# Five held weight slots, earlier turns, and low halves on ACT and GpSimd between the stages of a hybrid block

## The reference

```python
def first_block(...):
    ...
    h_res = h_res + rms_norm(m @ w_o[i], post_norm_g[i])      # 272 rows, 16 of them dropped at the end

def second_block(x, ...):
    for i in range(2):                                        # i = 0: GLA mixer, i = 1: MoBA mixer
        ...
        x = layer_norm_2(DEEPNORM_ALPHA * x + y, ln_g[i, 0], ln_b[i, 0])
        x = layer_norm_2(DEEPNORM_ALPHA * x + swiglu_ffn(x, ffn_w_gu[i], ffn_w_down[i]), ln_g[i, 1], ln_b[i, 1])
    return x

def swiglu_ffn(x, w_gu, w_down):
    gate, up = jnp.split(x @ w_gu, 2, axis=-1)
    return (jax.nn.silu(gate) * up) @ w_down
```

## Time and profile before

| | us |
|---|---|
| median of 3 launches | 913.05 |
| lowest and highest | 911.45, 913.55 |
| the profiled launch: its own time | 914.35 |
| the profiled launch: span from first to last instruction | 912.6 |
| PE busy in that span | 887.5 (97%) |
| DVE, ACT, POOL busy | 598.0, 422.0, 120.3 |
| mean granted clock of PE | 0.993 of full speed |

### The profile page before, as it was taken

How to read it: one execution, slowest core, us unless ns; L and a number is a source line. 1 busy time by engine, 2 the same in 40 slices (tenths; PEclk the granted TensorE clock), 3 DMA queues, 4 the chain that set the end, 5 groups by cost and what they waited for, 6 DMA issues and landing times.

```text
span 912.6 us, 14066 instructions
## 1 busy us (share of the span) xinstructions
PE 887.5 (97%) x5927; PEld 805.7 (88%) x5927; DVE 598.0 (66%) x845; ACT 422.0 (46%) x600; POOL 120.3 (13%) x106
## 2 busy tenths in 40 slices
PE   9999998999999999999999999989999999999995
PEld 7997998998887988879999988879977799999884
DVE  5997995687485684777555554576876765555436
ACT  5645453456652774526444443335553454444320
POOL 0343430122000311002000000015420200000000
PEclk9999998999999999999999999999999999999998
DMA  9753664563354752447665555466543656555631
GB/s 300 239 169 99 192 188 124 177 185 116 93 173 121 240 182 93 139 138 231 185 185 184 186 185 187 137 206 200 170 140 117 203 188 186 185 185 185 190 110 46
DMA packets 116009, 154.18 MB, mean 169 GB/s; under 512 B 5392, under 2 KB 91819, under 8 KB 115915
## 3 DMA queue, kind: packets, MB, share of 16 engines
q1 hardware_dynamic: 114218, 148.31, 51.9%
q0 software_dynamic: 1728, 4.98, 2.0%
HBM read 151.44 MB, written 1.05 MB: 167 GB/s over the span
## 4 chain that ended last, share of the span: by engine, by line
PE 87%; DVE 9%; ACT 1%; issue 1%; DMA 1%; DVEq 0%; SPq 0%
PE acc L572 25%; PE acc L573 24%; PE acc L574 24%; DVE w_lo L1548 2%; DVE conv L1693 2%; PE acc L637 2%; PE acc L638 1%; PE acc L640 1%; PE misc L708 1%; DVE y L1979 1%; PE misc L770 1%; ACT x_hi L1335 1%; PE acc L610 1%; DVE sc_acc L1713 1%; DMA x<-in_x 1%
## 5 line engine op out<-in xcount | busy, mean ns | idle before, releaser
L1548 DVE TENSOR_TENSOR w_lo<-staged,w_hi 128x1024 fp32r<-128x1024 f32 (+1 forms) x274 | 334.2, 1244 | 148.7 <-ACT w_hi L1140 147.8
L572 PE MATMUL acc<-x_hi,w_hi 128*128 128x256 f32 (+1 forms) x1288 | 367.5, 285 | 3.0 <-DVE m L1772 3.0
L573 PE MATMUL acc<-x_lo,w_hi 128*128 128x256 f32 (+1 forms) x1288 | 365.1, 283 | 0.0
L574 PE MATMUL acc<-x_hi,w_lo 128*128 128x256 f32 (+1 forms) x1288 | 362.6, 281 | 0.0
L1140 ACT CAST w_hi<-staged 128x1024 fp32r<-128x1024 f32 (+1 forms) x274 | 277.5, 1044 | 81.7 <-DMA staged<-in_ffn_w_down 46.8
L572 PEld LDWEIGHTS acc<-x_hi,w_hi 128*128 128x128 f32 x1288 | 243.0, 189 | 5.7 <-DVE m L1772 3.2
L574 PEld LDWEIGHTS acc<-x_hi,w_lo 128*128 128x128 f32 x1288 | 245.0, 190 | 0.0
L573 PEld LDWEIGHTS acc<-x_lo,w_hi 128*128 128x128 f32 x1288 | 243.6, 189 | 0.7 <-issue 0.2
L574 PE MATMUL acc<-w_hi,h_lo 128*128 128x512 f32 x176 | 69.6, 396 | 0.0
L572 PE MATMUL acc<-w_hi,h_hi 128*128 128x512 f32 x176 | 69.6, 395 | 0.0
L573 PE MATMUL acc<-w_lo,h_hi 128*128 128x512 f32 x176 | 69.6, 395 | 0.0
(11 more groups left out here) (371 smaller groups left out, 1197.8 us busy)
## 6 DMA issues: line engine op xcount, KB each, us to landing
staged<-in_ffn_w_gu SPq DMA_DIRECT2D x88, 512.0 KB, 3.6
staged<-in_w_in SPq DMA_DIRECT2D x58, 512.0 KB, 3.6
staged<-in_ffn_w_down SPq DMA_DIRECT2D x44, 512.0 KB, 4.1
staged<-in_gla_w_in SPq DMA_DIRECT2D x24, 512.0 KB, 3.7
staged<-in_moba_w_in SPq DMA_DIRECT2D x24, 512.0 KB, 3.9
staged<-in_w_o SPq DMA_DIRECT2D x8, 512.0 KB, 3.8
staged<-in_gla_w_out SPq DMA_DIRECT2D x8, 512.0 KB, 3.6
staged<-in_moba_w_out SPq DMA_DIRECT2D x8, 512.0 KB, 3.6
```

Of the source, the lines that this page charges most:

```text
L572: pe.matmul(dst, st_hi, mv_hi, start=start, stop=False)
L573: pe.matmul(dst, st_hi, mv_lo, start=False, stop=False)
L574: return pe.matmul(dst, st_lo, mv_hi, start=False, stop=stop)
L1548: nc.vector.tensor_tensor(lo, raw, hi, ALU.subtract).then_inc(split, 1)
```

## The change

1. `TAIL` becomes 5. In `n_product` the fourth slot of column half 0 is held too: after three slots for both tiles come slot 3 for tile 0, slots 4 to 7 for tile 0, and then slots 3 to 7 for tile 1. One semaphore, `tail_part`, counts the finished accumulators.
2. Turn 0 is issued inside the old stage, ahead of the last held slot of tile 1 (in `down0`: ahead of the last two slots of tile 1's half 1). Turn 1 opens `n_first`. Turn 2 stands between the two groups of low-half matmuls of tile 0, and turn 3 behind them. Within a tile all sixteen matmuls with `x_hi` now come ahead of the eight with `x_lo`.
3. The filler matmuls ahead of turns 0 and 2 are gone.
4. The low halves of tile 0 leave DVE: ACT copies the turned bank to `y` right behind the rounding, and POOL subtracts `x_hi` from it into `x_lo`.
5. The inverse root has one second-order step and one third-order step: five small instructions behind the seed in place of six, with other constants in the gain. In `w_o` two further small instructions become one.
6. DVE no longer takes column half 0 of both tiles in the middle of its weight splits, nor tile 1's half 0 inside tile 0's norm: `tail_norms` first norms tile 0 whole, and then takes tile 1. In `w_o` ACT's squares move in the same way.

```diff
@@ n_first
+                turn_rows(tag, 1)
                 open_out(name)
                 done = 4 * (int(tag[1]) - 1)
                 for t in range(TILES):
                     rows = slice(t * P, t * P + P)
-                    turn_rows(tag, 2 * t, 2)
-                    for j in range(2):
-                        pe.wait_ge(s["x_rounded"], done + 2 * t + j + 1)
-                        for part in range(2):
-                            if part == 1:
-                                if j == 0:
-                                    turn_rows(tag, 2 * t + 1, 0)
-                                await_read(pe, "%s_%d" % (tag, 2 * t + j))
+                    for part in range(2):
+                        for j in range(2):
+                            if part == 0:
+                                pe.wait_ge(s["x_rounded"], done + 2 * t + j + 1)
+                            elif t == 0:
+                                if j == 1:
+                                    turn_rows(tag, 2)
+                                pe.wait_ge(s["x_rest"], done // 2 + j + 1)
+                            else:
+                                await_read(pe, "%s_%d" % (tag, 2 + j))
...
+                    if t == 0:
+                        turn_rows(tag, 3)
@@ n_product
+                for q in range(3):
                     chunks_ready(q)
                     n_slots(stage, names, st_hi, st_lo, q, q + 1)
+                chunks_ready(3)
+                quarter(3, 0)
                 open_out(names[1])
...
+                for i in range(4, 8):
+                    quarter(i, 0)
+                for i in range(3, 8):
+                    if i == 7:
+                        turn_rows(tag, 0)
+                    quarter(i, 1)
@@ swiglu, PE
                             if t == 0 and hf == 0:
                                 down_ready(k)
+                            if layer == 0 and t == 1 and hf == 1 and k == FCH - 2:
+                                turn_rows("x3", 0)
                             mm = down_half(k, t, hf)
@@ ACT
+            for hf in range(2):
+                act.wait_ge(s["tail_part"], PARTS["w_o"] + hf + 1)
+                act.wait_ge(s["m_split"], 4)
+                squares(0, hf).then_inc(s["wo_ssq"], 1)
+            slot_done(act, "w_o", 3)
+            squares(1, 0).then_inc(s["wo_ssq"], 1)
...
+                if t == 0:
+
+                    nc.scalar.copy(y[:, 0, j * 512:j * 512 + 512], bank(name)).then_inc(read_sem(name), 1)
 
             def after_tail(stage, tag):
 
                 last = FIRST[stage] + COUNT[stage] - 1
+                round_rows(tag, 0)
+                if stage == "w_o":
+                    slot_done(act, "w_o", 7)
+                    squares(1, 1).then_inc(s["wo_ssq"], 1)
+                round_rows(tag, 1)
                 lead(Slot(last - 1, 0))
-                round_rows(tag, 0)
-                round_rows(tag, 1)
+                round_rows(tag, 2)
                 lead(Slot(last, 0))
-                round_rows(tag, 2)
                 round_rows(tag, 3)
@@ DVE
+                n = count(nc.vector.tensor_scalar(r.bitcast(I32), v.bitcast(I32), -0.5, ROOT_SEED, ALU.mult, ALU.add))
+                beside(0)
                 dve.wait_ge(dve_chain, n)
...
+                n = count(nc.vector.scalar_tensor_tensor(t, r, v, r, ALU.mult, ALU.mult))
+                beside(1)
+                dve.wait_ge(dve_chain, n)
+                link(nc.vector.scalar_tensor_tensor(r, t, -ROOT_A, r, ALU.add, ALU.mult))
+                link(nc.vector.scalar_tensor_tensor(t, r, v, r, ALU.mult, ALU.mult))
+                link(nc.vector.scalar_tensor_tensor(t, t, -ROOT_B, t, ALU.add, ALU.mult))
+                link(nc.vector.scalar_tensor_tensor(r, t, ROOT_C, r, ALU.add, ALU.mult))
...
+            def tail_norms(k, stage, first_half_done):
+
+                names = TAIL_OUTS[stage]
+                for hf in range(2):
+                    dve.wait_ge(s["tail_part"], PARTS[stage] + hf + 1)
+                    residual_moments(0, names[hf], hf)
+                norm_tile(k, 0)
+                first_half_done()
+                residual_moments(1, names[0], 0)
+                slot_done(dve, stage, COUNT[stage] - 1)
+                residual_moments(1, names[1], 1)
+                norm_tile(k, 1)
@@ POOL
+            def rest_tile0(tag):
+
+                for j in range(2):
+                    await_read(pool, "%s_%d" % (tag, j))
+                    nc.gpsimd.tensor_tensor(x_lo[:, 4 * j:4 * j + 4, 0:P], y[:, 0, j * 512:j * 512 + 512]
+                                            .rearrange("p (c r) -> p c r", c=4), x_hi[:, 4 * j:4 * j + 4, 0:P].bitcast(F32),
+                                            ALU.subtract).then_inc(s["x_rest"], 1)
```

163 lines of the change are left out of this document (56 added, 107 removed).

## The result

| | before | changed |
|---|---|---|
| median, us | 913.16 (4 launches) | 902.81 (4 launches, 900.99 to 904.25) |
| ratio, 95% interval | | 0.9889 [0.9867, 0.9911] |
| profiled launch: own time, span | 914.35, 912.6 | 904.15, 902.4 |
| granted clock of PE, share of full speed | 0.993 | 0.992 |

The change makes the kernel 10.4 us faster. The prediction was 895.3 with a range up to 900.5: some 7.5 us of the forecast gain are missing.

The account below looks back on a forecast made before the run. PE, busy 887.5 of 912.6 us, was taken as the bound. Four places save 17.8, less 2.55 of waits at turn 2, plus 2.45 at the end: 17.7 us, giving 895.3 us against the median of 913.05; range 892.3 to 900.5.

Parts of the forecast that it names:

- PE as the bound: Whole kernel: PE works 887.5 of 912.6 us, so only its idle time and unused work can shorten it much.
- the stretches at the four places: Behind w_o, gla_out, down0 and moba_out: 69.47 us falls to 4 x 12.9 = 51.6 with turns unwaited, saving 17.8.
- the wait at turn 2: PE waits 0.85 us for tile 1's x behind gla_out, down0 and moba_out, 2.55 in all; none counted in w_o.
- no wait of PE for weights: Inside the stages: PE never waits for splits or loads; the rival that weights are the limit, near 913, has chance 0.02.
- the end: Program's end: the last x starts 4.43 to 4.5 us behind PE's end in place of 6.94, gaining 2.45.
- "Just in time" for turn 0: Behind the old stage's held matmuls: x due at T + 5.24, or 5.6 behind gla_out and moba_out; turn at T + 5.6.
- the first rival (turn 0 late): Late x stops the six held matmuls too: about 2.1 us each behind gla_out and moba_out, 899.5 us; chance 0.10.
- the clock rival: Without fillers and with waits at turn 2, PE's clock falls once or twice: 898.4 to 901.5 us; chance 0.12.
- The 0.7 for POOL beside DVE: In tile 1's norm: POOL's subtraction slows DVE's two centrings to 0.57 of their pace, losing 0.7 us a place.
- Weight loads: The extra held slot frees 5.6 us later; load, rounding and split take 6.0, hidden with some ten us of cover.

Follow-up runs that it names:

- e2: The changed kernel with ACT's first copy of q for MoBA moved ahead of the weight cast queued there; 902.92 us, ratio 0.9880.
- e6: The changed kernel with four slots in place of five kept for tile 1 in down0 and down1; 905.66 us, ratio 0.9926.
- e13: e11 plus POOL's second subtraction of tile 0 waiting for tile 1's second centring, behind gla_out, down0 and moba_out; 897.72 us, ratio 0.9830.
- e1: The changed kernel with tile 1's low-half matmuls in n_first in pairs again, ahead of the next high-half ones; 896.49 us, ratio 0.9832.
- e4: The changed kernel with POOL issuing the swap of k ahead of its rotation of q, for all pairs of heads; 898.93 us, ratio 0.9838.
- e11: The changed kernel with the swap of k issued ahead of POOL's rotation of q for the first two MoBA heads alone; 897.63 us, ratio 0.9831.
- e12: The changed kernel with both e1's pairs and e11's early swap of k for the first two heads; 896.91 us, ratio 0.9821.
- e14: The kernel before with ACT copying MoBA's first two heads of q five times in place of once; 920.12 us, ratio 1.0064.
- e15: The changed kernel with SP holding the twelfth MoBA q and k weight load until the first swap of q has landed; 903.55 us, ratio 0.9890.
- e3: The changed kernel with the third load of gain and shift moved behind the MoBA swaps; 901.36 us, ratio 0.9857.

## Why the prediction was wrong

**Right, by its steps.** PE as the bound; the stretches at the four places (12.90, 14.10, 14.18 and 13.90, foretold as 12.9 and 13.75, in all 0.9 too low); the wait at turn 2, 0.84, foretold as 0.85; no fall of the clock at the turns; no wait of PE for weights; the end, 4.53 foretold as 4.43 to 4.5. "Just in time" for turn 0 was just that: on the pace in `w_o` and `moba_out`, 0.16 and 0.23 late behind `gla_out` and `down0`, 1.01 late in `down0` in e2's execution, and 1.05 late with one slot less (e6), as the same sum says. So the first rival (turn 0 late) came true in small, and it is not what is missing; the clock rival did not come true in its place at the turns.

**Right in size, wrong in kind.** The 0.7 for POOL beside DVE was taken from rows 7 as a common slowdown to 0.57. It measured 0.66, but as a wait until POOL's instruction was done: one centring took 1.40 and the other 0.74, where the prediction has both at 1.1 to 1.3. That the sizes agree is luck of the place. On a small root instruction the pace would have said next to nothing, and 1.14 was lost (e13).

**The step that failed** is "Weight loads": "Hidden, with some ten us of cover." I asked of the new release times only whether PE would get its weights, and with "The trace has not one wait of PE for a split or a load inside the stages" I closed the matter. Both sentences are true, and neither is the question. The loads have other customers. ACT waits for them with MoBA's copy of q behind it in its list, and they share the DMA engines with two swaps of 32 KB. The chain through this copy and these swaps ended 0.35 us behind PE already. I had the moved matmuls of tile 1 in my list of edits and priced them at their place, at nothing; their true price is the time at which four slots come free. The terms of the sum add up to 17.7, and at the places that they name 16.8 was gained (69.47 less the 55.08 of the four places, and 2.4 at the end). Some 7.9 were given back at one matmul, 5.05 as idle time and the rest as clock, and the program's start was 1.3 shorter in this execution: 10.2 in the profiled launches. It is outside my range since I had no case of this kind in it. The "clock falls" rival gave 898.4 to 901.5 and has the second half of the mechanism, but puts it at the turns and leaves out the idle time itself.

**What is shown and what is not.** Shown: the stall goes when the order of the low halves is undone (e1: one trace and three of four launches), and when the swap of k leaves the chain (e4, e11, e12); it comes in the kernel before when the copy alone is late (e14); the landing of a swap hangs on the loads beside it (e15); one link alone does not decide (e2, e15). Open: whether the fifth slot has any part in it (four slots and the pairs were not tried together), why the copy of q came at 6.78 in one execution and at 8.37 in another (e4, e3) behind the same releases, and why one launch of e1 took 904.

**A faster version.** e1, e11 and e12 all have lower medians than the changed kernel: 896.5 to 897.6 against 902.8, and 913.2 to 913.5 for the kernel before on their chips; the intervals of e11 and e12 lie clear of the changed kernel's, that of e1 does not. The plain one is e1, whose edit is one line; e11 had the narrowest launches (896.87 to 897.94), and its remedy does not hang on when the copy comes. They are what the prediction forecast for the change, 895.3, within 1.2 to 2.3 us.

## What to carry to other kernels

When a change moves the moment at which buffers come free, ask not only whether the engine at the bound still gets its data, but what every other engine that waits for these transfers has queued behind that wait, and which small transfers share the DMA engines with them. A wait of 0.35 us on the bounding engine is worth a row of its own in the working: it marked a chain without slack, and 2.52 us at that chain's start cost 6.97 at its end. And a gain that is there at one mark has to be followed to the next ones: five differences between marks showed what the total of 10 us hid.
